# A feed-forward's downward product with two levels of Strassen's recursion in the place of one

## The reference

```python
def feed_forward(h):                       # h: 1024 tokens x 1024
    hn = rms_norm(h, norm_mlp_w)
    u = jnp.square(jax.nn.relu(hn @ w_up)) # w_up: 1024 x 4096
    return h + u @ w_down                  # w_down: 4096 x 1024
```

## Time and profile before

| | us |
|---|---|
| median of three runs (3703.58 to 3706.09) | 3704.13 |
| span of the profiled execution | 3703.5 |
| TensorE busy in it | 3572.4 |
| VectorE busy | 2195.4 |
| ScalarE busy | 1275.9 |
| POOL busy | 1045.1 |
| feed-forward, down product of the first 512 tokens | 194.7 |
| feed-forward, down product of the second 512 tokens | 194.3 |
| after the last matmul | 11.5 |

### The profile page before, as it was taken

How to read it: one execution, slowest core, us unless ns; L and a number is a source line. 1 busy time by engine, 2 the same in 40 slices (tenths; PEclk the granted TensorE clock), 3 DMA queues, 4 the chain that set the end, 5 groups by cost and what they waited for, 6 DMA issues and landing times. The chain is left out here.

```text
span 3703.5 us, 52577 instructions
## 1 busy us (share of the span) xinstructions
PE 3572.4 (96%) x20084; PEld 2408.0 (65%) x20084; DVE 2195.4 (59%) x4339; ACT 1275.9 (34%) x2406; POOL 1045.1 (28%) x981
## 2 busy tenths in 40 slices
PE   7999999999999999989999999999989999999998
PEld 4656556798744655477987577556565686458743
DVE  4377455764775377557656652774388645764565
ACT  3255434632722355356335222663323211001100
POOL 2400154666642300356656140004054000000000
PEclk9999999999999999999999999999999999999999
DMA  5101241002021110110020301000001323542354
GB/s 196 49 18 41 85 153 62 2 18 76 2 83 69 51 41 18 57 35 2 18 76 35 120 18 46 24 2 22 23 24 57 114 91 124 194 170 81 114 179 151
DMA packets 108983, 253.77 MB, mean 69 GB/s; under 512 B 5216, under 2 KB 33888, under 8 KB 108352
## 3 DMA queue, kind: packets, MB, share of 16 engines
q1 hardware_dynamic: 102624, 230.28, 17.8%
q10 hardware_dynamic: 4816, 14.16, 1.0%
q0 software_dynamic: 1296, 5.97, 0.4%
HBM read 223.14 MB, written 27.26 MB: 68 GB/s over the span
## 5 line engine op out<-in xcount | busy, mean ns | idle before, releaser
L1003 PE MATMUL ps<-ring,hT 128*128 128x512 f32 (+3 forms) x1296 | 374.2, 445 | 9.7 <-DVE nrm_b L1184 4.4
L1003 PEld LDWEIGHTS ps<-ring,hT 128*128 128x128 f32 x1296 | 217.2, 191 | 145.2 <-issue 121.3
L1544 DVE TENSOR_REDUCE stat_a<-ps 128x1 f32<-128x1280 f32 (+1 forms) x144 | 190.7, 1366 | 154.0 <-PE ps L1388 154.0
L1442 PE MATMUL ps<-hT,ring 128*128 128x512 f32 (+1 forms) x640 | 280.2, 551 | 0.0
L1753 POOL TENSOR_TENSOR P_b<-P_b,stat_b 128x1280 f32<-128x1280 f32 (+1 forms) x108 | 227.8, 2130 | 176.0 <-DVE stat_b L1769 137.3
L2779 PE MATMUL ps<-Wd,const 128*128 128x512 f32 x384 | 185.7, 592 | 0.0
L1484 ACT ACTIVATE YT<-ps,stat_a 128x1280 f32<-128x1280 f32 (+1 forms) x144 | 176.6, 1232 | 25.4 <-DVE stat_a L1544 25.4
L2669 PE MATMUL ps<-Y 128*128 128x256 f32 x768 | 171.1, 379 | 0.9 <-DVE Y L2654 0.5
L1528 POOL COPY rb_a<-stat_a 128x64 f32<-128x64 f32 x72 | 14.6, 236 | 539.0 <-DVE YT L1557 539.0
L2669 PEld LDWEIGHTS ps<-Y 128*128 128x128 f32 x768 | 145.8, 190 | 21.3 <-issue 1.5
L2798 ACT ACTIVATE hid<-hid 128x1024 f32<-128x1024 f32 x32 | 33.8, 1057 | 317.0 <-DVE hid L2872 317.0
(11 more groups left out here) (583 smaller groups left out, 8005.2 us busy)
## 6 DMA issues: line engine op xcount, KB each, us to landing
ring<-in_w_down SPq DMA_DIRECT2D x32, 2048.0 KB, 7.9
ring<-in_w_up SPq DMA_DIRECT2D x16, 2048.0 KB, 8.5
ring<-in_w_in SPq DMA_DIRECT2D x14, 2048.0 KB, 8.1
adaw_b<-in_w_ada SPq DMA_DIRECT2D x16, 1024.0 KB, 5.2
ring<-in_w_out SPq DMA_DIRECT2D x6, 2048.0 KB, 7.9
ring<-in_w_in SPq DMA_DIRECT2D x6, 1536.0 KB, 7.0
gates<-const SPq DMA_DIRECT2D x32, 256.0 KB, 2.4
x<-res SPq DMA_DIRECT2D x16, 512.0 KB, 3.9
```

Of the source, the lines that this page charges most:

```text
L1003: mm = pe.matmul(ps[:, bank(n), 0:hi - lo], hT[:, k, t * P:(t + 1) * P], w[:, k, lo:hi], start=(k == 0), stop=(k == KC - 1))
L1442: mm = pe.matmul(ps[:, GB, 0:hi - lo], pr.view(i0 + c)[:, k, b % 4 * P:(b % 4 + 1) * P], hT[:, k, lo:hi], start=(k == 0), stop=(k == KC - 1))
L1544: dve.tensor_reduce(st[:, i % 4, m:m + 1], scored_at(i, m), AX, ALU.max, negate=True)\
```

## The change

The feed-forward's upward product stays. The downward product of a half becomes a two-level one: the first level splits the 512 tokens x 4096 hidden x 1024 columns into 2x2 blocks of 256 tokens, 2048 hidden rows and 512 columns, which gives seven passes (`PASSES`), and each pass is itself a product in seven, over 2x2 blocks of 128 tokens and 256 columns, in two chunks of eight row blocks. So a half has 7 passes x 2 chunks x 7 products x 4 matmuls of 256 columns. Each pass ends in PSUM (at the places of `up_place`, two sets alternating); VectorE puts its four blocks together (`keep_pass`, from PSUM) and adds them into the result (`add_result`), which stands in `hT`, where ScalarE has loaded the residual rows.

The sums are made in four places. Four of the seven passes need a first-level sum of hidden blocks, made in place on VectorE (`mix_operand`, two halves of 128x2048). Four need a first-level sum of weights: these are made once for the whole kernel, in `stage_diff` of the first layer, unit by unit of 128 rows (16 units): SP loads two blocks of 512 KB of `w_down`, POOL makes four sums of 128x512 in place (`sum_blocks`), SP stores the 1 MB to a DRAM tensor `down_sums`, and then loads the next unit into the same tile. The second-level sums are made per chunk: four of 128x512 of the hidden blocks (`mix_hidden`) and two of 128x1024 of the weights (`mix_down`) on VectorE, and two of 128x1024 of the weights on POOL, each behind one of VectorE's. POOL had no work in this stage. There are 28 downward chunks in the place of 32, each of eight row blocks by 512 columns, 2 MB.

The core of the diff (in `stage_diff`, on SP and POOL; then what is new in `stage_mlp`):

```diff
+            def load_blocks(u):
+                if u:
+                    sp.wait_ge(*S["sums_stored"](16 * u))
+                for k in range(2):
+                    sp.dma_start(sums["buf"][:, k], sums["src"](u, k)).then_inc(*S["params_in"].inc(16))
+            def store_sums(u):
+                sp.wait_ge(*S["sums"](4 * (u + 1)))
+                sp.dma_start(sums["dst"](u), sums["buf"][:].rearrange("p k n -> p (k n)")).then_inc(*S["sums_stored"].inc(16))
+            if sums:
+                load_blocks(0)
+            for s in range(n + 1):
+                for i, (b, lo, hi) in enumerate(pieces):
+                    if done_by[i] != s:
+                        continue
+                    sp.wait_ge(*S["gate_kept"](i + 1))
+                    sp.dma_start(spill[:, b, lo:hi], raw[:, i % 2, 0:hi - lo]).then_inc(*S[f"gate_spilled_{i % 2}"].inc(16))
+                    if i in chunk_ends:
+                        pr.load(sp, i0 + chunk_ends.index(i) + SLOTS)
+                u = (s - 5) // 2
+                if sums and s % 2 and 0 <= u < sums["n"]:
+                    store_sums(u)
+                    if u + 1 < sums["n"]:
+                        load_blocks(u + 1)
...
+            def sum_blocks(u):
+                pool.wait_ge(*S["params_in"](32 * (u + 1)))
+                pool.tensor_tensor(b00, b01, b00, ALU.subtract).then_inc(*S["sums"].inc())
+                pool.wait_ge(*S["sums"](done + 1))
+                pool.tensor_tensor(b01, b11, b01, ALU.subtract).then_inc(*S["sums"].inc())
+                pool.wait_ge(*S["sums"](done + 2))
+                pool.tensor_tensor(b11, b11, b00, ALU.subtract).then_inc(*S["sums"].inc())
+                pool.wait_ge(*S["sums"](done + 3))
+                pool.tensor_tensor(b10, b11, b10, ALU.subtract).then_inc(*S["sums"].inc())
             for pair in range(n // 2):
                 pool.wait_ge(*S["combined"](halves_combined(2 * pair + 1)))
...
                 ins.then_inc(*S["rb_ready"].inc())
                 if pair:
                     scaled(pair - 1)
+                if sums and pair < sums["n"]:
+                    sum_blocks(pair)
             scaled(n // 2 - 1)
...
+PASSES = (1, 2, 5, 7, 6, 3, 4)
+DOWN_CHUNKS = 2 * len(PASSES)
...
+                freed(pe, q - 2)
+                for c in range(2):
+                    e = DOWN_CHUNKS * half + 2 * (i - PAIRS) + c
+                    pr.arrived(pe, i0 + down_chunk(e))
+                    pe.wait_ge(*S["tokens_mixed"](e + 1))
+                    A, B, M, T = hidden(e), down_weights(e), Al[e % 2], Wl[e % 2]
+                    factors = {1: (A[0][0], B[0][0]), 2: (A[0][1], B[1][0]), 3: (M[3], B[1][1]), 4: (A[1][1], T[2]),
+                               5: (M[0], T[0]), 6: (M[1], T[1]), 7: (M[2], B[0][1])}
+                    for x in UP_ORDER:
+                        if x == 2:
+                            give_back()
+                        if x in (5, 6):
+                            pe.wait_ge(*S["weights_mixed"](2 * e + x - 4))
+                        if x in (7, 4):
+                            pe.wait_ge(*S["sums"](2 * e + (1 if x == 7 else 2)))
+                        a, b = factors[x]
+                        for g in range(4):
+                            mm = pe.matmul(at(q, x), a[:, g, :], b[:, g, :], start=(c == 0 and g == 0 and x % 2 == 1),
+                                           stop=(c == 1 and g == 3), skip_group_check=True)
...
+        @block.gpsimd
+        def _(pool):
+            for e in range(2 * DOWN_CHUNKS):
+                B, T = down_weights(e), Wl[e % 2]
+                pool.wait_ge(*S["weights_mixed"](2 * e + 1))
+                pool.tensor_tensor(B[0][1], B[1][1], B[0][1], ALU.subtract).then_inc(*S["sums"].inc())
+                pool.wait_ge(*S["weights_mixed"](2 * e + 2))
+                pool.tensor_tensor(T[2], T[1], B[1][0], ALU.subtract).then_inc(*S["sums"].inc())
...
+            during = {2: 5, 4: 7, 6: 6, 8: 3}
...
+                for i in range(1, DOWN_CHUNKS):
+                    if i + 1 < DOWN_CHUNKS:
+                        mix_hidden(e0 + i + 1)
+                    if i % 2 == 0:
+                        keep_pass(half, i // 2 - 1)
+                    if i in during:
+                        mix_operand(half, during[i], 0)
+                    if i + 1 < DOWN_CHUNKS:
+                        mix_down(e0 + i + 1)
+                    if i in during:
+                        mix_operand(half, during[i], 1)
+                    if i % 2:
+                        if i >= 3:
+                            add_result(half, (i - 3) // 2)
+                        if half == 0 and i == 11:
+                            mix_tokens()
...
+                keep_pass(half, NP - 1)
+                add_result(half, NP - 1)
```

More of the change, by code:

```diff
@@ L1371, in _ @@
         def _(sp):
[L1372 to L1376, removed]
+            def load_blocks(u):
[21 more added lines that the diff above has]
+                        load_blocks(u + 1)
+            if sums:
+                sp.wait_ge(*S["sums_stored"](16 * sums["n"]))
         @block.tensor
@@ L2676, in stage_mlp @@
     i0 = pr.next_use
-    Hc, Wu, Wd, Hd, tmp, xt = (mix[k] for k in ("tokens", "up", "down", "hidden", "sums", "x"))
+    Hc, Wu, Wl, Al, tmp, U, R, us, xt = (mix[k] for k in ("tokens", "up", "weights", "hidden", "sums", "kept", "result", "parts", "x"))
+    SA = mix["tokens_flat"].rearrange("p (f n) -> p f n", f=FF // 2 // P)
     HALF = BANK // 2
     PAIRS = FF // (2 * P)
[L2681 to L2711, removed]
+    NP = len(PASSES)
@@ L2713, in tokens, with up_chunk, down_chunk, at @@
+    STEPS = PAIRS + NP
+    def up_chunk(n):
+        return n // PAIRS * (PAIRS // 2 + DOWN_CHUNKS) + n % PAIRS // 2
+    def down_chunk(e):
+        return e // DOWN_CHUNKS * (PAIRS // 2 + DOWN_CHUNKS) + PAIRS // 2 + e % DOWN_CHUNKS
+    def at(q, x):
+        bank, cols = up_place(q, x)
+        return ps[:, bank, cols]
+    def up_weights(n):
+        return up_blocks(pr.view(i0 + up_chunk(n)), n)
     def tokens(half):
         return token_blocks(hT, half)
-    def hidden(j, pair):
-        return [[hid[:, 2 * j + g, (2 * pair + t) * P:(2 * pair + t + 1) * P] for g in range(2)] for t in range(2)]
+    def operand(x):
+        low, high = slice(0, FF // 2 // P), slice(FF // 2 // P, FF // P)
+        one, two = slice(0, HALF), slice(HALF, BANK)
+        return {1: hid[:, low, one], 2: hid[:, high, one], 3: hid[:, high, one], 4: hid[:, high, two],
+                5: SA, 6: SA, 7: hid[:, low, two]}[x]
@@ new lines, in hidden, with down_weights, freed @@
+    def hidden(e):
+        L = operand(PASSES[e % DOWN_CHUNKS // 2])
+        c = e % 2
+        return [[L[:, 8 * c + a:8 * c + 8:2, b * P:(b + 1) * P] for a in range(2)] for b in range(2)]
+    def down_weights(e):
+        w = pr.view(i0 + down_chunk(e))
+        return [[w[:, a:8:2, n * HALF:(n + 1) * HALF] for n in range(2)] for a in range(2)]
+    def freed(eng, q):
+        half, i = divmod(q, STEPS)
+        if i < PAIRS:
+            eng.wait_ge(*S["rows_kept"](PAIRS * half + i + 1))
+        else:
+            eng.wait_ge(*S["combined"](NP * half + i - PAIRS + 1))
@@ L2912, in stage_mlp, with mix_hidden @@
-    pr.end(chunk)
+            def mix_hidden(e):
+                half, i = divmod(e, DOWN_CHUNKS)
+                A, M = hidden(e), Al[e % 2]
+                if e >= 2:
+                    dve.wait_ge(*S["product_done"](e - 1))
+                if i < 2:
+                    dve.wait_ge(*S["kept_by_act"](PAIRS * half + PAIRS // 2))
+                else:
+                    dve.wait_ge(*S["kept_by_act"](PAIRS * (half + 1)))
+                step(dve.tensor_tensor(M[0], A[1][0], A[1][1], ALU.add))
+                dve.tensor_tensor(M[2], A[0][0], A[1][0], ALU.subtract)
+                step(dve.tensor_tensor(M[1], M[0], A[0][0], ALU.subtract))
+                dve.tensor_tensor(M[3], A[0][1], M[1], ALU.subtract).then_inc(*S["tokens_mixed"].inc())
```

334 lines of the change are left out of this document (186 added, 148 removed).

## The result

The changed kernel takes 3730.61 us (median of 4 runs, 3728.17 to 3732.97) against 3705.11 before (4 runs); the ratio is 1.0065, with a 95% interval of 1.0053 to 1.0077. It is slower by some 25 us. The forecast of 3702 us (3668 to 3725) was too low. Of the prediction's three cases "slower than 3711.5", with a chance of 0.30, came out, and the time lies above the range.

The account below looks back on a forecast made before the run. PE bounded the old kernel; in the changed downward halves the SBUF port shared by VectorE and POOL would. 3703.5 − 24 (feed-forward) + 22 (differential attention) = 3701.5, with 0.6 to the median 3702 us; range 3668 to 3725.

Parts of the forecast that it names:

- slower than 3711.5: Whole kernel: a measured time above 3711.5 us, made up of "The slower chain" and "full blocking"; chance 0.30.
- the port: Feed-forward downward passes: POOL's and VectorE's two-input SBUF reads alternate, so a pass takes 27.4 us against PE's 24.2.
- the residual loads: Start of each downward half: four loads of 512 KB delay the first weights by 1 to 2.4 us.
- The gap: Between the two feed-forward halves: 2.1 us without PE work, forecast to go as two PSUM sets alternate.
- full blocking: Rival, feed-forward: each POOL sum holds the port 2.35 us, not 2.08; gain only 12, total 3713.5 us; chance 0.08.
- the price of the sums in the differential attention: First layer's differential attention: transfers and sums delay scale copies and PE's transposes, costing 22 us in all.
- the ring load: Differential attention, at 310 us: a store stands behind this load, costing 5.4 us.
- The following pair absorbs it: Differential attention: each 2.0 us delay is absorbed by the next pair, so every second of eleven pairs pays, 11 us.
- The slower chain: Rival, differential attention: store, load and sums cost the upper end, 33 us, feed-forward gains only 15; 3721 us; chance 0.22.
- No port limit: Rival, feed-forward: POOL's operations fit between VectorE's, PE stays the bound, gain 57; total 3669 us; chance 0.13.
- cheap transfers: Rival, differential attention: transfers overlap better or POOL's sums are faster, costing 9 instead of 22; 3689 us; chance 0.17.
- store plus load below 8.2 and the regular stall is gone: Differential attention: with a unit's store and load together under 8.2 us, the regular stall vanishes, leaving 8 us.

Follow-up runs that it names:

- the run with the chain alone: The changed kernel with each unit's four POOL sums replaced by equally long fills that read nothing, loads and stores kept, feed-forward reading plain blocks: 3717.98 us.

## Why the prediction was wrong

**The feed-forward was right, term by term.** PE loses an eighth of the downward matmuls, VectorE alone would keep up, and the port is the bound: the sums gave 188.1 (before 1 to 2.4 for the residual loads) and 183.3 us, the trace shows 189.05 and 183.80. The passes, too: the chain that ended last has VectorE's result additions (start, us)

```profile
3204.85 3.38 DVE hT L2994
...
3232.38 3.38 DVE hT L2994
...
3259.91 6.68 DVE hT L2994 x2
...
3288.71 6.67 DVE hT L2994 x2
```

that is 27.5 us from pass to pass for the forecast 27.4, and 28.8 for 28.6 where a pass has two additions. The gap is gone, and the tail is 5.70 us for the forecast 5.5. Together 23.9 for 24. The handover with 0.13 us of overlap, not "full blocking", gave these numbers. The run with the sums on VectorE shows the reason, too: without POOL the second half takes 169.28 us, the forecast's 169.4 for PE alone. One small term stays unproven: no run leaves out the residual loads, to which the prediction charged 1 to 2.4 us; the halves came 0.95 and 0.5 us over its sums without them.

**The step that failed is the price of the sums in the differential attention: 22 forecast, 49.6 measured.** Its chain was drawn rightly, and with the port out of the way so was its idle time: PE waits 23.5 us for scale copies for the forecast 22, in the run with the chain alone six times for 2.0 to 3.2 us in every second pair (13.3 for the forecast 11), 4.5 behind the ring load (for 5.4) and 5.7 in the last pairs (for 5.6). It is partly luck that the sum comes so near: 0.6 us of the forecast's 2.0 a stall stood for the port, which is away there. The transfers, too: in the change's first turn store and load took 5.0 and 5.2 us, the upper ends, but over all units the medians from issue to landing are near the 4.6 (load) and 4.2 (store) of the forecast:

```profile
down_a<-in_w_down SPq DMA_DIRECT2D x32, 512.0 KB, 4.5
down_sums<-down_a SPq DMA_DIRECT2D x16, 1024.0 KB, 4.2
```

Two terms were missing or far too small:

- *The clock, taken at nothing.* I charged a stall with its idle time. In the windows read behind two of them TensorE ran at a granted clock of 0.57 to 0.88; in the change PE was busy 13.6 us longer, and in the run with the chain alone 13.0 us longer, with the same matmuls. Rows of before had no such stall in this stage, but they show PE at 0.66 in the idle tail, and I took nothing from that.
- *The port, a second time.* I added POOL's time to VectorE's in the feed-forward from rows that I knew, and in the differential attention gave it 0.6 us ("16.9 where a VectorE sum holds the port"). POOL's sums there hit the combination of the maps, 1.68 us stretched to 2.76 or 3.79, on whose result PE waits directly; the scale copy was held as well, 1.63 us for 0.41. On top of the chain's 36.2 the port costs 13.4 us and brings the stage to 49.6; without the stores it costs 29.3.

So the bounds of 8 to 33 us were too narrow: they varied the length of transfers and of POOL's operations and never asked which VectorE operation POOL's new reads would meet, nor whether PE restarts at full speed. "The following pair absorbs it" held for the scale copies, but not for the whole: in the change two pairs took some 37.5 us, as from the transpose at 222.55 to the one at 260.05, against 29.8.

**The rivals.** The slower chain had the right sign and place, and at 3721 the nearest time, but not by its reason: at the upper end of the transfers it asked for 33 us of waiting, and the chain alone made 23.5 us of it. "No port limit" and "cheap transfers" are refuted: halves of 184 to 189 us, and a run without any store that still loses 27 us. The threshold "store plus load below 8.2 and the regular stall is gone" held for the copies and not for the time, as the run without stores shows.

**What stays open.** The stage's parts were told apart by replacing operations, and each is read from one execution; the division of the port's 13.4 us goes by what ended PE's waits there. Why the gaps grow when the clock is kept up, and why the port costs less beside the long chain than without the stores, is not shown.

## What to carry to other kernels

Work for POOL, though POOL is idle, is priced by what it does to VectorE, which shares its port, at the moment at which it runs: ask which two-input VectorE operation it meets and who waits for that one. Here VectorE had the room, and giving it POOL's two sums of a chunk, 1.22 us each, beat leaving them to POOL by 29 us. A background job that is queued in the same list as a step of the critical path, behind its own transfers, belongs one round later, where its data are there already; here that was one line and 45 us.

## What was not expected of the hardware

A stall of about the same length brought the clock down in one place and not in another. In the run with the chain alone, PE stood for 2.0 us until 221.48 and for 2.1 us until 288.20. The transposes that ended the stalls, and the windows around them:

```profile
221.48 0.33 PE L1442 MATMUL ps<-const,rb_a 128*128 128x128 f32 x1 [2.01 <-POOL rb_a L1563]
...
288.20 0.33 PE L1442 MATMUL ps<-const,rb_a 128*128 128x128 f32 x1 [2.06 <-POOL rb_a L1563]
```

```profile
220.00:224.00 4.00, 2.52 (x41) 2.33 (x41) 1.11 (x2) 0.41 (x1) 1.84 (x4) 1.00 0.73 293
224.00:228.00 4.00, 4.00 (x32) 2.47 (x29) 2.40 (x2) 1.86 (x3) 0.00 (x0) 1.00 0.43 143
...
288.00:292.00 4.00, 3.80 (x36) 3.66 (x38) 0.00 (x0) 0.00 (x0) 0.56 (x2) 0.59 0.79 323
```

After the first the clock stays at 1.00, after the second it is 0.59. The pair that ends with the stall and the pair behind it show what that costs. Around the first stall the two took 31.99 us (from the transpose at 204.43 to the one at 236.42), which is the 29.8 of before and the stall to within 0.2. Around the second they took 33.73 us (271.09 to 304.82), 1.9 more than that. So the price of a single short stall can't be read off its length here; over the stage it was 13.0 us beside 23.2 us of added idle time. Why the two differ is open.
